# Expert stage of a two-block model: a width of token columns for each unit instead of one width for all

## The reference, cut to what matters

```python
def moe_swiglu(h, w_router, w_gate, w_up, w_down):
    xt = h.reshape(b * t, d)                         # 1024 tokens, d = 1024
    logits = (xt @ w_router).astype(jnp.float32)     # 8 experts
    top_logits, top_idx = lax.top_k(logits, TOP_K)   # TOP_K = 2
    gates = jax.nn.softmax(top_logits, axis=-1)
    ...
    hid = (jax.nn.silu(lax.ragged_dot(xs, w_gate, group_sizes))
           * lax.ragged_dot(xs, w_up, group_sizes))  # 3584 hidden features
    ys = lax.ragged_dot(hid, w_down, group_sizes)
    ...
    out = jnp.einsum('nk,nkd->nd', gates.astype(y.dtype), y)
```

## Time and profile before

| what | value |
| --- | --- |
| median of 3 runs | 6184.69 us (6181.36 to 6188.75) |
| profiled execution | 6181.93 us, span 6180.2 us |
| PE busy | 5687.9 us (92% of the span) |
| ACT, DVE, POOL busy | 18%, 20%, 2% |
| expert stage on PE, first transpose to last | about 3575 to 6111 us |
| one unit in it | 315.5 us (starts of `up` at 3903.14 and 4218.66) |
| DMA in the expert stage | about 150 GB/s |

### The profile page before, as it was taken

One profiled execution on the slowest core, in us unless ns is written; L12 is line 12 of the kernel. 1 busy time (PEld: TensorE's weight loads), 2 busy tenths in 40 slices (PEclk: granted clock), 3 DMA queues, 4 the chain that ended last, 5 costly groups with the idle time before them and its releaser, 6 DMA issues. The chain is left out here.

```text
span 6180.2 us, 55822 instructions
## 1 busy us (share of the span) xinstructions
PE 5687.9 (92%) x22275; PEld 3869.5 (63%) x22275; DVE 1210.5 (20%) x2244; ACT 1091.6 (18%) x1892; POOL 107.8 (2%) x110
## 2 busy tenths in 40 slices
PE   7688898999899999898999589999999999999995
PEld 3344443445444448743566468888888888888884
DVE  3223321334300000021455211010101110101002
ACT  3321101123200000073244111111111111111111
POOL 0000000000000000000000100000000000000001
PEclk9889999999999999999999699999999999999997
DMA  4024001220011111133221044545454545454545
GB/s 175 28 89 167 0 0 63 104 92 34 25 41 34 41 58 38 39 124 121 79 79 59 21 152 137 173 139 166 136 169 141 168 134 168 143 170 135 164 144 185
DMA packets 660687, 638.81 MB, mean 103 GB/s; under 512 B 17363, under 2 KB 595922, under 8 KB 658514
## 3 DMA queue, kind: packets, MB, share of 16 engines
q1 hardware_dynamic: 647888, 593.00, 30.7%
q0 software_dynamic: 8288, 27.29, 1.2%
q10 hardware_dynamic: 4386, 16.82, 0.7%
HBM read 541.62 MB, written 95.45 MB: 103 GB/s over the span
## 5 line engine op out<-in xcount | busy, mean ns | idle before, releaser
L2836 PE MATMUL psum<-arena 128*128 128x272 f32 x7168 | 1646.4, 393 | 6.9 <-issue 6.9
L2836 PEld LDWEIGHTS psum<-arena 128*128 128x128 f32 x7168 | 1362.4, 190 | 289.5 <-issue 8.8
L2851 PE MATMUL psum<-arena 128*128 128x272 f32 x3584 | 831.9, 392 | 0.0
L2851 PEld LDWEIGHTS psum<-arena 128*128 128x128 f32 x3584 | 676.6, 190 | 136.0
L1060 PE MATMUL psum<-arena 128*128 128x512 f32 x1408 | 607.3, 594 | 5.2 <-DMA arena<-in_ffn_w_up 5.2
L1060 PEld LDWEIGHTS psum<-arena 128*128 128x128 f32 x1408 | 268.5, 191 | 343.4 <-issue 343.4
L2769 DVE TENSOR_TENSOR arena<-arena,psum 128x512 f32 x224 | 154.1, 688 | 1504.3 <-ACT arena L2789 1504.3
L998 PE MATMUL psum<-arena 128*128 128x256 f32 (+1 forms) x1664 | 419.6, 416 | 17.9 <-DMA arena<-in_ffn_w_down 13.7
L998 PEld LDWEIGHTS psum<-arena 128*128 128x128 f32 x1664 | 319.0, 192 | 118.4 <-issue 76.8
L1276 PE MATMUL psum<-arena 128*128 128x512 f32 (+1 forms) x680 | 297.3, 595 | 2.4 <-PEq L99 2.4
L2789 ACT ACT_TABLE_LOAD x112 | 143.7, 1283 | 862.9 <-PE psum L2836 862.9
(11 more groups left out here) (403 smaller groups left out, 4455.0 us busy)
## 6 DMA issues: line engine op xcount, KB each, us to landing
arena<-in_moe_w_gate SPq DMA_DIRECT2D x112, 1024.0 KB
arena<-in_moe_w_up SPq DMA_DIRECT2D x112, 1024.0 KB
arena<-in_moe_w_down SPq DMA_DIRECT2D x64, 1792.0 KB, 8.3
y_dram<-zeros SPq DMA_DIRECT2D x1, 22528.0 KB, 69.5
arena<-in_c_w_in SPq DMA_DIRECT2D x8, 2048.0 KB, 10.8
y_dram<-arena ACTq DMA_DIRECT2D x8, 2048.0 KB, 6.6
arena<-in_ab_w_in SPq DMA_DIRECT2D x7, 2048.0 KB, 8.1
z_dram<-arena SPq DMA_DIRECT2D x52, 256.0 KB, 2.2
```

The lines of the kernel that those rows point to most:

```text
L2836: last = nc.tensor.matmul(g.ps[:, 2 * f + a, 0:N], wup[b][:, k, a * 256 + f * P:a * 256 + (f + 1) * P], xt[:, k, 0:N], start=(k == 0), sto ...
L2851: last = nc.tensor.matmul(g.ps[:, 4 + b, 0:N], wdn[b][:, k, :], hid[:, k, 0:N], start=(k == 0), stop=(k == EF_T - 1))
```

## The change

The router stage no longer computes one width. It writes each unit's own count of tokens, held between 1 and 512, into a second row of `g.table`. The expert stage on PE has one loop over the units. At the head of each unit it reads that unit's count from the table and `pick` chooses a body by it: a binary tree of `If`/`Else`, five levels deep, over 32 widths. The widths are closer: every 4 columns from 228 to 292. The units then run at N = 240, 252, 264, 272, 248, 260, 268 and 256 in this order, if the counts are those of the reference.

```diff
-GRAIN = 16
...
-            step(v.tensor_tensor(past, cnt_u.unsqueeze(2).broadcast_to([P, MAX_UNITS, UNIT // GRAIN - 1]), steps_of.unsqueeze(1).broadcast_to([P, MAX_UNITS, UNIT // GRAIN - 1]), ALU.is_gt))
-            step(v.tensor_reduce(vu, past, AX.X, ALU.add))
-            step(v.tensor_scalar(vu, vu, 1.0, None, ALU.add))
+            step(v.tensor_scalar(vu, cnt_u, 1.0, None, ALU.max))
+            step(v.tensor_scalar(vu, vu, float(UNIT), None, ALU.min))
             step(v.tensor_scalar(eidx, eidx, float(NE - 1), None, ALU.min))
             step(v.tensor_copy(g.table[:, 0, :], eidx))
-            step(v.tensor_reduce(tot[:, 0:1], vu, AX.X, ALU.max))
-            step(v.tensor_copy(g.width, tot[:, 0:1]))
+            step(v.tensor_copy(g.table[:, 1, :], vu))
...
-WIDTHS = (16, 17, 18, 19, 20, 22, 24, 28, 32)
+WIDTHS = (16, 32, 64, 96, 128, 160, 192, 208, 220, *range(228, 293, 4), 304, 320, 352, 384, 448, UNIT)
...
-            width = pe.value_load(g.width[0:1, 0:1], min_val=1, max_val=UNIT // GRAIN)
...
-            def every_unit(N):
+            def one_unit(u, N):
                 nb = -(-N // P)
-                with pe.Fori(0, n) as u:
-                    up(u, N)
-                    for d in range(NB_DN):
-                        down(u, d, N)
-                        if d in X_AFTER:
-                            turn_x(u + 1, X_AFTER[d])
-                        if d:
-                            turn_y(u, d - 1, nb)
-                    turn_y(u, NB_DN - 1, nb)
-
-            def pick(j):
-                if j == len(WIDTHS) - 1:
-                    every_unit(WIDTHS[j] * GRAIN)
+                up(u, N)
+                for d in range(NB_DN):
+                    down(u, d, N)
+                    if d in X_AFTER:
+                        turn_x(u + 1, X_AFTER[d])
+                    if d:
+                        turn_y(u, d - 1, nb)
+                turn_y(u, NB_DN - 1, nb)
+
+            def pick(u, tokens, a, b):
+
+                if b - a == 1:
+                    one_unit(u, WIDTHS[a])
                     return
-                with pe.If(width > WIDTHS[j]):
-                    pick(j + 1)
+                mid = (a + b) // 2
+                with pe.If(tokens > WIDTHS[mid - 1]):
+                    pick(u, tokens, mid, b)
                     pe.nop()
                 with pe.Else():
-                    every_unit(WIDTHS[j] * GRAIN)
+                    pick(u, tokens, a, mid)
+                    pe.nop()
...
-            pick(0)
-            pe.nop()
+            with pe.Fori(0, n) as u:
+                tokens = pe.value_load(g.table[0:1, 1, ds(u, 1)], min_val=1, max_val=UNIT)
+                pick(u, tokens, 0, len(WIDTHS))
```

More of the change, by code:

```diff
@@ L2567, in router_stage @@
     iu, row, eidx, cnt_u, vu = S.at(656, MAX_UNITS), S.at(672, MAX_UNITS, NE), S.at(768, MAX_UNITS), S.at(784, MAX_UNITS), S.at(800, MAX_UNITS)
-    row2, tot = S.at(816, MAX_UNITS, NE), S.at(912, 2)
+    row2 = S.at(816, MAX_UNITS, NE)
     w12, gr, zero_i = S.at(920, NT, 2), S.at(936, MAX_UNITS, 8), S.at(1032, ID_SLOTS // P).bitcast(U32)
-    steps_of, past = S.at(1100, UNIT // GRAIN - 1), S.at(1140, MAX_UNITS, UNIT // GRAIN - 1)
     tok_i = g.tok_ids
@@ L2581, in _ @@
             nc.gpsimd.iota(iu, [[1, MAX_UNITS]], base=0, channel_multiplier=0, allow_small_or_imprecise_dtypes=True)
-            nc.gpsimd.iota(steps_of, [[GRAIN, UNIT // GRAIN - 1]], base=GRAIN, channel_multiplier=0, allow_small_or_imprecise_dtypes=True)
             nc.gpsimd.iota(tok_i, [[P, NT]], base=0, channel_multiplier=1)
@@ L3013, in program @@
         g.tok_ids, g.idx = sb("tok_ids", NT, dt=U32)[:, :], sb("idx", 4, dt=U32)[:, :]
-        g.table, g.n_units = sb("table", 1, MAX_UNITS, dt=I32)[:, :, :], sb("n_units", 1, dt=I32)[:, :]
-        g.width = sb("width", 1, dt=I32)[:, :]
+        g.table, g.n_units = sb("table", 2, MAX_UNITS, dt=I32)[:, :, :], sb("n_units", 1, dt=I32)[:, :]
         g.zeros = sb("zeros", ZERO_W)[:, :]
```

## The result

| | before | after |
| --- | --- | --- |
| median | 6183.02 us (6181.07 to 6188.75, 4 runs) | 6295.29 us (6293.31 to 6299.61, 4 runs) |
| ratio | 1 | 1.0184, 95% interval [1.017, 1.0199] |
| profiled execution, span | 6181.93, 6180.2 us | 6295.07, 6293.3 us |

The kernel became 112.3 us slower. 6251 had been forecast, with a range of 6195 to 6325.

A forecast was written before the change was run, and what follows sets the result against it. The expert stage was taken as bound by PE alone. Savings of 135.5 us against 202 us of cost gave +66.5 on the profiled 6181.93, 6248.4; with 2.8 for the median, 6251 us, range 6195 to 6325.

The forecast's parts named there:

- the third rival: PE's tree: a following jump queues behind the code fetch ahead; 3.81 us more on 19 jumps, 72 us, 6323; chance 0.15.
- narrower columns, transposes: Expert stage on PE: 116 columns fewer save 131 us, 32 transposes fewer in turn_y save 3.5 us.
- router, start of the stage: Router on DVE: fewer small steps save 1.2 us if the chain behind is exposed; 1 us taken.
- new jumps: PE's choice of body: 45 new exposed jumps to code not held, at 3.81 us each, cost 171.5 us.
- reads and compares: Head of each unit on PE: reading the count, compares and moves cost 1.1 us a unit, 9 us in all.
- clock: PE after each of seven idle gaps: lower granted clock loses 3.1 us each time, 21.5 us in all.
- The count of jumps: PE's tree and unit loop: 3 exposed jumps ahead of the first unit, 43 between units; 46 replace one.
- The two rows of jumps without their code: Earlier source view, line 2870: two jumps over bodies took 3808 and 3722 ns, basis for 3.81 us a jump.
- over 4 us a jump: Gaps between units on PE: longer than 4 us a jump would mean fetches ahead delay following jumps.
- The other signs: Profile after: over 1 MB of instruction fetches, PE busy about 110 us less, gaps of 17 to 33 us, longest before units 3 and 8.
- The first (jumps nearly free): PE's choice: 46 jumps at 0.22 us plus 9 cost 19 us, no clock lost, 6068 us; chance 0.09.
- The second (exits fold): PE's tree: the inner exit leads straight out, 34 new jumps, 129.5 us, total 6209; chance 0.08.

The follow-up runs named there:

- the sweep: The changed kernel with experts sorted by count and 14 width classes whose bodies PE runs through in program order, without the tree: 6075.06 us, ratio 0.9823.
- three_levels: The changed kernel with eight widths instead of 32, so a tree of three levels instead of five: 6214.93 us, ratio 1.0056.
- store_late: The changed kernel, but ACT stores a unit to y_dram only after the first group of the next unit's up: 6273.94 us, ratio 1.0147.
- straight: Against the kernel before: eight bodies of fixed widths one behind the other, no choice, unit loop or jump; right only for these counts: 6040.38 us, ratio 0.977.
- tree_one_width: The changed kernel with its tree, but the router writes the fullest unit's count for every unit, so all run at 272 columns: 6430.93 us, ratio 1.0403.
- sweep4: The sorted kernel that runs through the bodies in program order, with classes every 4 columns from 292 to 228: 6116.11 us, ratio 0.9891.

## Why the prediction was right, and what it undersized

The sign, the mechanism and the place were right. The sum was 46 us short, nearly all of it in one term, the price of a jump. 6295 lies between the forecast (6251) and the third rival (6323), and nearer to the rival. That the range held it is owed to that rival, whose mechanism had been given a chance of 0.15. Against the terms of the sum:

| term | forecast | measured | from |
| --- | --- | --- | --- |
| narrower columns, transposes | -134.5 | -133 | lengths of units in the sweep, below |
| router, start of the stage | -1 | -2.9 | first transpose 3572.38 against 3575.29 |
| new jumps | +171.5 | +222 | 45 took 225.9, before 3.8 |
| reads and compares | +9 | +10 | gaps 238.6 - 6.9 less the jumps |
| clock | +21.5 | +16 | the units after are 117 us shorter in sum, not 133 |
| sum | +66.5 | +112 | medians 6295.3 - 6183.0 |

The start of the stage is a reading of two executions and not shown to be the router's: with the same router the first transpose stands at 3568.71 us in `three_levels` and at 3573.86 in `store_late`.

**The columns.** In the sweep, which has no jumps between them, the second unit of 272 columns takes 315.08 us and the next, of 264, takes 306.12 (from one start to the next, less the gap in between; the start behind it is below): 8.96 / 8 = 1.12 us a column, where 1.13 was forecast.

```profile
4540.12 199.62 PE L2856 MATMUL psum<-arena 128*128 128x264 f32 x896 [0.45 <-issue]
```

116 x 1.12 and the 3.5 us of transposes are the 133 of the table. `straight` shows the whole gain at once, 141 us, of which some 8 come from missing loop branches and the earlier start. The weight load stays hidden at 240 columns; `up` of the sweep's last unit takes 203 ns a matmul, against 202 computed:

```profile
5729.53 181.70 PE L2856 MATMUL psum<-arena 128*128 128x240 f32 x896 [0.90 <-issue]
```

**The count of jumps.** 46 had been counted, 45 waited for their code, and each gap held the number that I had given it, but for one. (Of the 46, 38 follow another, not 39 as the third rival has it, which changes nothing.)

**The price of a jump.** This is the step that was mis-sized: "The two rows of jumps without their code agree within 3%, and I take them." They agreed because both were alone. 45 jumps at 3.81 us are 171.5 us, and they took 225.9, 54 more. 25 of these are the store's: the second jump of each gap is 3.6 us dearer beside it, and `store_late` shows that. I had written that the last exit lies beside the store, and had not asked what the store does to the other seven.

The remaining 29 us come nearly all from jumps in a row. One that follows another directly costs 4.8 us. In the gap ahead of unit 3 eight jumps fetched 16 blocks, as I read it one for the target and one for the code behind it, mostly started within 0.5 us of each other. Behind the read of the table, where about 1 us passes between two jumps, the price is down to 3.9 on average. That is the third rival's mechanism, at about 1 us for each following jump and not 3.8 on every second. No run took the look-ahead away, so this cause is read from the trace and not shown. The sign that I had named for it, over 4 us a jump, has come: 5.0 us, and 4.5 in `store_late` with the store moved away (203.0 us for 45).

**The clock.** The gaps between units (22 to 42 us) each cost about 2 us, less than the 3.1 I had taken from the earlier trace rows. The unit ahead of which stood 41.35 us:

```profile
4233.00:4239.00 6.00, 5.92 (x18) 0.68 0.01 3
4239.00:4245.00 6.00, 6.00 (x28) 1.00 0.00 0
```

18 matmuls began in its first 6 us, against 14 there. In the seven stretches of 6 us from a unit's first matmul on the granted clock was 0.56 to 0.73, which comes to 32 us at half the clock, 16 us lost. The length of the pause made no difference that I can see: 0.59 behind 22.42 us and 0.73 behind 22.11, 0.69 behind 41.35 and 0.58 behind 41.61.

**The other signs.** The queue of instructions moved 132 blocks, 2.16 MB, in the stage (over 1 MB forecast), PE is busy 120 us less (110), and the gaps between units are 22 to 42 us (17 to 33), longest ahead of units 3 and 8 as forecast.

**The rivals.** The first (jumps nearly free) would have needed the back jump's 0.22 us everywhere; the back jump itself now takes 4.6 us and more. It is not the distance: with 8 bodies in the program instead of 32 (`three_levels`) it takes 4.6 to 4.9 us behind another jump beside no store, and 3.7 us where it comes first. The second (exits fold) is out, as each gap has all its exits. By the Trainium skill's rule in "Runtime: NRT & Kernel Launch", section on instruction fetch mechanics, a taken branch outside the code that is held waits for a fetch; the trace agrees in 45 cases, and `tree_one_width` shows that what was fetched a unit ago is gone.

## What to carry to other kernels

What a jump in PE's program costs hangs on whether the code at its target is held: 0.2 us here if it was, 3.3 to 5 us if not, whereas eight bodies of straight code cost nothing. So put what is chosen at run time into the order of the code (sort the work, sweep once), and count the taken jumps of a tree, entries and exits, before its leaves are made finer. Look also at the jumps behind the last piece of work: in `sweep4` four of them outlasted the store that was to hide them, by 13 us. And look at what other engines send to the DMA queues in just that moment: a 2 MB store raised the price of one jump from 4.8 to 8.4 us.

## What was not expected of the hardware

- A code fetch queues behind a bulk store: a jump took 8.2 to 8.6 us beside the store of 2 MB at 380 GB/s, 4.9 without it. The store was delayed as well, 10.1 us to landing against 6.6 before.
- Jumps in a row cost 4.8 us each, a lone one 3.3 to 3.8.
- Behind a pause of 41 us the clock came back no later than behind one of 22, or of 14: the granted clock of the first 6 us was 0.69 and 0.58 behind 41 us, 0.59 and 0.73 behind 22, and 0.51 in the earlier trace rows.
